# Fourier sums folded four ways, with the folds in the projection, and one block for the sample's and the prompt's Fourier part and the output projection

## The reference

```
h    = layer_norm(x) * (1 + sc1) + sh1
q, k, v, u = split(h @ w_in)                     # 512 columns each
o    = diff_attention(rope(q), rope(k), v)       # 4 heads of 128, then rms norm * gain
f    = fft2(u in 4 groups of 128, ortho).real    # over positions and group channels
f    = f @ w_fourier[group]
mix  = concat(o, f) @ w_out
x    = layer_norm(ALPHA * x + (1 + g1) * mix) * ln1_g + ln1_b
h    = layer_norm(x) * (1 + sc2) + sh2
x    = layer_norm(ALPHA * x + (1 + g2) * ((silu(h @ w_gate) * (h @ w_up)) @ w_down)) * ln2_g + ln2_b
```

## Time and profile before

| what | value |
|---|---|
| median of three runs | 3462.7 us (3454.75 to 3465.51) |
| profiled execution, its own time | 3461.79 us |
| its span | 3460.0 us |
| PE busy | 3147.7 us, 91% of the span |
| DVE busy | 1497.7 us, 43% |
| ACT busy | 1039.3 us, 30% |
| POOL busy | 1041.9 us, 30% |
| DMA | 309.29 MB, mean 89 GB/s |

### The profile page before, as it was taken

The page is one execution under the profiler, slowest core; times in us unless marked ns, Lnnn a source line. Parts: engine busy times, 40 slices in busy tenths (PEclk is TensorE's granted clock), DMA queues, the critical chain, the costliest instruction groups (busy, mean ns, idle before and its releaser), DMA issues.

```text
span 3460.0 us, 39737 instructions
## 1 busy us (share of the span) xinstructions
PE 3147.7 (91%) x15230; PEld 2628.0 (76%) x15230; DVE 1497.7 (43%) x2226; ACT 1039.3 (30%) x1592; POOL 1041.9 (30%) x589
## 2 busy tenths in 40 slices
PE   8799996999999967598599999979999998999995
PEld 1588884666666646477499999969999987999994
DVE  2343333888888734477521222171221245221225
ACT  1111112777777723223321211121121122111211
POOL 0122220011111110266443333373333345333333
PEclk9899998999999989799799999989999998999997
DMA  9222226121211032444431111232111213121111
GB/s 354 85 92 94 94 89 140 31 60 48 69 50 47 22 111 101 156 146 161 158 106 61 61 61 66 92 116 74 66 61 61 100 59 122 62 70 62 61 61 49
DMA packets 165031, 309.29 MB, mean 89 GB/s; under 512 B 12725, under 2 KB 100662, under 8 KB 162870
## 3 DMA queue, kind: packets, MB, share of 16 engines
q1 hardware_dynamic: 164922, 307.85, 27.0%
HBM read 241.69 MB, written 66.11 MB: 89 GB/s over the span
## 4 chain that ended last, share of the span: by engine, by line
PE 44%; POOL 3%; issue 2%; DVE 1%; POOLq 1%; ACT 0%; DMA 0%; DVEq 0%; SPq 0%; ACTq 0%
PE ffn_gu L1737 10%; PE ffn_gu L1738 10%; PE ffn_gu L1739 10%; PE ffn_dn L1753 5%; PE ffn_dn L1754 5%; PE ffn_dn L1755 5%; POOL ffn_out L1670 1%; POOL ffn_h_lo L1710 1%; POOL ffn_w_lo L1659 1%; POOLq L1665 1%; DVE ffn_out L1780 0%; DMA ffn_h_in<-scr_h_d 0%; POOL ffn_a_lo L1688 0%; DVE ffn_h_lo L1784 0%; ACT ffn_w_hi L1607 0%
## 5 line engine op out<-in xcount | busy, mean ns | idle before, releaser
L1737 PE MATMUL ffn_gu<-ffn_h_hi,ffn_w_hi 128*128 128x384 f32 x2112 | 707.3, 335 | 28.6 <-DVE ffn_h_lo L1784 25.5
L1739 PE MATMUL ffn_gu<-ffn_h_hi,ffn_w_lo 128*128 128x384 f32 x2112 | 706.9, 335 | 0.0
L1738 PE MATMUL ffn_gu<-ffn_h_lo,ffn_w_hi 128*128 128x384 f32 x2112 | 706.8, 335 | 0.0
L1659 POOL TENSOR_TENSOR ffn_w_lo<-ffn_w_raw,ffn_w_hi 128x2048 fp32r<-128x2048 f32 x99 | 461.0, 4657 | 405.7 <-ACT ffn_w_hi L1607 403.9
L1799 DVE TENSOR_TENSOR ffn_a_raw<-ffn_sil,ffn_gu 128x384 f32<-128x384 f32 x132 | 73.1, 554 | 949.2 <-PE ffn_gu L1739 949.2
L1737 PEld LDWEIGHTS ffn_gu<-ffn_h_hi,ffn_w_hi 128*128 128x128 f32 x2112 | 397.3, 188 | 30.8 <-issue 25.8
L1738 PEld LDWEIGHTS ffn_gu<-ffn_h_lo,ffn_w_hi 128*128 128x128 f32 x2112 | 397.3, 188 | 1.2
L1739 PEld LDWEIGHTS ffn_gu<-ffn_h_hi,ffn_w_lo 128*128 128x128 f32 x2112 | 397.3, 188 | 0.0
L1753 PE MATMUL ffn_dn<-ffn_w_hi,ffn_a_hi 128*128 128x512 f32 x792 | 315.4, 398 | 47.3 <-DVE ffn_total L1811 16.5
L1811 DVE TENSOR_TENSOR ffn_total<-ffn_total,ffn_dn 128x512 f32<-128x512 f32 x360 | 246.0, 687 | 229.8 <-PE ffn_dn L1755 229.8
L867 DVE TENSOR_REDUCE att_peak<-att_sc 128x1 f32<-128x1024 f32 x256 | 312.5, 1221 | 71.8 <-PE att_sc L693 65.9
(11 more groups left out here) (216 smaller groups left out, 4578.7 us busy)
## 6 DMA issues: line engine op xcount, KB each, us to landing
ffn_w_raw<-in_w_gu SPq DMA_DIRECT2D x132, 512.0 KB, 4.5
ffn_w_raw<-in_w_dn SPq DMA_DIRECT2D x66, 512.0 KB, 4.5
mod_wa<-in_w_ada SPq DMA_DIRECT2D x32, 768.0 KB, 7.0
att_q_t<-scr_qs_d SPq DMA_DIRECT2D x128, 128.0 KB, 2.9
proj_x_in<-in_x SPq DMA_DIRECT2D x18, 512.0 KB, 3.8
mix_x_in<-in_x SPq DMA_DIRECT2D x18, 512.0 KB, 4.0
scr_x_d<-mix_x SPq DMA_DIRECT2D x18, 512.0 KB, 4.7
scr_h_d<-mix_h SPq DMA_DIRECT2D x18, 512.0 KB, 5.5
```

The costliest lines, as they stand in the source:

```text
L1659: nc.gpsimd.tensor_tensor(w_lo[:, i, :], w_raw[:, i, :], w_hi[:, i, :].bitcast(F32), ALU.subtract).then_inc(wlo_done[i], 1)
L1737: nc.tensor.matmul(dst, w_hi[:, i, cols], h_hi[:, k, tokens], start=(k == 0), stop=False)
L1738: nc.tensor.matmul(dst, w_hi[:, i, cols], h_lo[:, k, tokens], start=False, stop=False)
L1739: m = nc.tensor.matmul(dst, w_lo[:, i, cols], h_hi[:, k, tokens], start=False, stop=(k == KD - 1))
```

## The change

The sample's rows are put in another order on the host (`sample_rows`; the rotary table and the output follow). Four consecutive tiles k of the sample then hold rows n, n + 1024, 1024 - n and 2048 - n (n below 512; for n = 0 the last two are rows 512 and 1536). `project` keeps u of four tiles, and DVE (`fold_even`) and POOL (`fold_odd`) add and subtract them into four operands, which go to `fold_d`; row 512 and a running sum for output position 1024 are kept apart (`b0_d`, `mid_d`). The Fourier sums of the sample are then 4 parts (even cosine, even sine, odd cosine, odd sine) of 4 chunks of 128 rows with tables of 512 columns, in place of 32 steps. Two chunks of the prompt come before them in the same list (`CHUNKS` = 18).

`attention` copies each finished quad twice out of `ring`, exact and rounded, and POOL subtracts; the hi and the lo part are stored. So the attention half of the mixed operand is loaded already split.

`fourier_sample`, `fourier_prompt` and `mix_out` become one block, `fourier_and_mix`. Its result of the Fourier part stays in SBUF. The load and split of `w_out` lie between the chunks. For the output projection the sample's tiles come first and the prompt's last. The attention half of a tile's product (`products(t, 0)`) doesn't wait for a split; the Fourier half (`products(t, 1)`) does. `x_in` and `x1_n` have one buffer in place of two, and the loops are written out. The tables' low parts are made by POOL in place of DVE.

The core of the diff:

```diff
...
+            def store_fold(k):
+                sp.wait_ge(odd_done, k + 1)
+                sp.wait_ge(mid_done, k + 1)
+                for part in range(4):
+                    whole = part == 1 or k
+                    sp.dma_start(fold_d[part, k, 0 if whole else 1:P, :], u[0 if whole else 1:P, part, :]).then_inc(fold_stored, 16)
+                if k == 0:
+                    for part, row in ((0, 0), (2, 1), (3, 3)):
+                        sp.dma_start(fold_d[part, 0, 0:1, :], pair[0:1, row, :]).then_inc(fold_stored, 16)
+                    sp.dma_start(b0_d, pair[0:1, 2, :]).then_inc(fold_stored, 16)
...
+                if t > PT and (t - PT) % 4 == 0:
+                    store_fold((t - PT) // 4 - 1)
...
+                if t > PT and (t - PT) % 4 == 0:
+                    act.wait_ge(fold_stored, 64 * ((t - PT) // 4 + 1))
+                nc.scalar.activation(u[:, t if t < PT else (t - PT) % 4, :], acc[:, 3, :], ACT.Copy).then_inc(u_done, 1)
...
+            def fold_odd(k):
+                pool.wait_ge(u_done, PT + 4 * (k + 1))
+                if k:
+                    pool.wait_ge(fold_stored, 64 * (k + 1))
+                nc.gpsimd.tensor_tensor(pair[:, 1::2, :], u[:, 0::2, :], u[:, 1::2, :], ALU.subtract).then_inc(minus_done, 1)
+                pool.wait_ge(minus_done, k + 1)
+                pool.wait_ge(plus_done, k + 1)
+                nc.gpsimd.tensor_tensor(u[:, 2, :], pair[:, 1, :], pair[:, 3, :], ALU.subtract)
+                nc.gpsimd.tensor_tensor(u[:, 3, :], pair[:, 1, :], pair[:, 3, :], ALU.add).then_inc(odd_done, 1)
+                pool.wait_ge(even_done, k + 1)
+                if k:
+                    pool.wait_ge(mid_done, k)
+                    nc.gpsimd.tensor_tensor(mid[:], mid[:], u[:, 0, :], ALU.add).then_inc(mid_done, 1)
+                else:
+                    nc.gpsimd.tensor_copy(mid[:], u[:, 0, :]).then_inc(mid_done, 1)
...
+            def fold_even(k):
+                dve.wait_ge(u_done, PT + 4 * (k + 1))
+                if k:
+                    dve.wait_ge(fold_stored, 64 * (k + 1))
+                nc.vector.tensor_tensor(pair[:, 0::2, :], u[:, 0::2, :], u[:, 1::2, :], ALU.add).then_inc(plus_done, 1)
+                dve.wait_ge(plus_done, k + 1)
+                dve.wait_ge(minus_done, k + 1)
+                nc.vector.tensor_tensor(u[:, 0, :], pair[:, 0, :], pair[:, 2, :], ALU.add)
+                nc.vector.tensor_tensor(u[:, 1, :], pair[:, 0, :], pair[:, 2, :], ALU.subtract).then_inc(even_done, 1)
...
+                    sp.wait_ge(flo_done, m + 1)
+                    for part, tile in ((0, f_hi), (1, f_lo)):
+                        src = tile[:, m % 2, :].bitcast(F32)
...
-                        nc.scalar.activation(f_out[:, m % 2, :], ring[:], ACT.Copy, scale=keep["subln_g"][:, 0:1]).then_inc(ring_read, 1)
+                            act.wait_ge(stored[m % 2], 32 * (m // 2))
+                        nc.scalar.activation(f_raw[:, m % 2, :], ring[:], ACT.Copy, scale=keep["subln_g"][:, 0:1])
+                        nc.scalar.activation(f_hi[:, m % 2, :], ring[:], ACT.Copy, scale=keep["subln_g"][:, 0:1]).then_inc(ring_read, 1)
...
+            def split_out(m):
+                pool.wait_ge(ring_read, place["z", m] + 1)
+                nc.gpsimd.tensor_tensor(f_lo[:, m % 2, :], f_raw[:, m % 2, :], f_hi[:, m % 2, :].bitcast(F32),
+                                        ALU.subtract).then_inc(flo_done, 1)
...
-def fourier_sample(nc, keep, u_d, w_f, chan, tab_s, four_d):
-def fourier_prompt(nc, keep, u_d, w_f, chan, tab_p, four_d):
-def mix_out(nc, keep, x, att_d, four_d, w_out, mod_rows, ln_g, ln_b, x1_d, h2_d):
...
+CHUNKS = PT + 4 * 4
...
+def fourier_and_mix(nc, keep, x, fold_d, b0_d, mid_d, up_d, w_f, chan, tab_p, tab_s, signs, att_d, w_out, mod_rows, ln_g, ln_b, x1_d, h2_d):
...
+        x_in = s.sb("x_in", [P, D])
+        x1_n = s.sb("x1_n", [P, D])
...
+        ORDER = list(range(PT, NT)) + list(range(PT))
...
+            def load_chunk(i):
+                part, k = chunk_place(i)
+                if i >= 3:
+                    sp.wait_ge(oplo_done, i - 2)
+                sp.dma_start(op_raw[:, i % 3, :], up_d[k] if part == PROMPT_SET else fold_d[part, k]).then_inc(op_landed[i % 3], 16)
+                if i >= 3:
+                    sp.wait_ge(tablo_done, i - 2)
+                sp.dma_start(tab_raw[:, i % 3, :], tab_p[k] if part == PROMPT_SET else tab_s[part, k]).then_inc(tab_landed[i % 3], 16)
...
+            def load_m(r):
+                if r >= 2:
+                    sp.wait_ge(acc_done, r - 1)
+                for part, tile in ((0, m_hi), (1, m_lo)):
+                    sp.dma_start(tile[:, r % 2, 0:HEADS, :].bitcast(F32),
+                                 att_d[part].rearrange("h c (t q) -> t c h q", q=P)[ORDER[r]]).then_inc(m_landed[r % 2], 16)
...
+            sp.dma_start(chan_in, chan.rearrange("t p c -> p t c")).then_inc(small_landed, 16)
+            sp.dma_start(wf_in.rearrange("p (g d) -> p g d", g=GROUPS), w_f.rearrange("g p d -> p g d")).then_inc(small_landed, 16)
+            load_chunk(0)
...
+            for i in range(1, CHUNKS):
+                load_chunk(i)
+                if i % 2 and i // 2 < KD:
+                    load_w(i // 2)
+                if i == 8:
+                    load_x(0)
+                    load_gate(1)
                     sp.dma_start(norm_b[:], ln_b.to_broadcast([P, D])).then_inc(row_landed, 16)
+                if i == 12:
+                    sp.wait_ge(chunk_used, PT + 1)
+                    load_m(0)
+                    load_m(1)
...
+            for r in range(NT + 2):
+                if r == ST:
+                    sp.wait_ge(gated, ST)
+                    load_gate(0)
+                if r + 1 < NT:
+                    load_x(r + 1)
+                if r + 2 < NT:
+                    load_m(r + 2)
...
+                for g in range(GROUPS):
+                    rows = slice(g * P, (g + 1) * P)
+                    dst = bank[:, base + g, :]
+                    stop = k == (PT - 1 if part == PROMPT_SET else 3)
+                    nc.tensor.matmul(dst, op_hi[:, i % 3, rows], tab_hi[:, i % 2, :], start=(k == 0), stop=False)
+                    nc.tensor.matmul(dst, op_hi[:, i % 3, rows], tab_lo[:, i % 2, :], start=False, stop=False)
+                    if part == 0 and k == 0:
...
+                        nc.tensor.matmul(dst, b0_hi[:, rows], across, start=False, stop=False)
+                        nc.tensor.matmul(dst, b0_lo[:, rows], across, start=False, stop=False)
+                    m = nc.tensor.matmul(dst, op_lo[:, i % 3, rows], tab_hi[:, i % 2, :], start=False, stop=stop)
+                m.then_inc(chunk_used, 1)
...
+            def products(t, half):
+                slot = t % 2
+                if half == 0:
+                    pe.wait_ge(m_landed[slot], 32 * (t // 2 + 1))
+                    if t < 2:
+                        pe.wait_ge(direct_done, 2 * GROUPS)
+                    else:
+                        pe.wait_ge(gated, t - 1)
+                else:
+                    pe.wait_ge(mlo_done, t + 1)
...
+            for i in range(CHUNKS):
+                sums(i)
+                if i == 0:
+                    mix_middle()
+                for part in (PROMPT_SET, 0, 1, 2):
+                    if i == last_chunk(part) + 2:
+                        mix_channels(part)
+            products(0, 0)
+            products(1, 0)
+            mix_channels(3)
+            products(0, 1)
+            products(1, 1)
+            for t in range(2, NT + 2):
+                if t < NT:
+                    products(t, 0)
+                    products(t, 1)
+                turn(t - 2)
...
+            def split_table(i):
+                pool.wait_ge(tabhi_done, i + 1)
+                nc.gpsimd.tensor_tensor(tab_lo[:, i % 2, :], tab_raw[:, i % 3, :], tab_hi[:, i % 2, :].bitcast(F32),
+                                        ALU.subtract).then_inc(tablo_done, 1)
...
+            def combine(par):
+                base = first_bank(2 * par + 1)
+                dve.wait_ge(direct_done, GROUPS * (par + 1))
+                for g in range(GROUPS):
+                    dve.wait_ge(mixed, GROUPS * (2 * par + 2) + g + 1)
+                    first = 1 - par
+                    near, far = slice(0, 256), slice(256 + first, 512)
+                    back = slice(511 - first, None if par else 0, -2)
+                    nc.vector.tensor_tensor(f_all[:, g, 0, par:512:2], direct[:, g, near], bank[:, base + g, near], ALU.subtract)
+                    nc.vector.tensor_tensor(f_all[:, g, 3, par + 2 * first:512:2], direct[:, g, first:256],
+                                            bank[:, base + g, first:256], ALU.add)
+                    nc.vector.tensor_tensor(f_all[:, g, 2, back], direct[:, g, far], bank[:, base + g, far], ALU.subtract)
```

(40 more changed lines are left out.)

773 lines of the change are left out of this document (328 added, 445 removed).

## The result

The changed kernel takes 3385.95 us (median, 3382.57 to 3388.22) against 3462.98 for the kernel before on the same chip: ratio 0.978, 95% interval 0.9763 to 0.9799. The profiled execution took 3382.57 us with a span of 3380.5. The forecast was 3367, range 3335 to 3415. The sum was not right term by term, though, and that is what follows.

The account below looks back on a forecast made before the run. PE was taken to bound projection and attention; 105 of 432 us in the merged blocks were waits and slow clock. -110.1 + 1 + 4.5 + 8.4 + 1.7 = -94.5 from 3461.8 gives 3367 us, range 3335 to 3415.

Parts of the forecast that it names:

- (e): Projection: folds cost 0 to 1.5 us at each of three tiles, 1 taken; last store lands 4.5 us later.
- (f): Attention: a second copy out of `ring` adds 14 x 0.6 = 8.4 us; at the end 1.7 us more.
- (a): Start of the new block: from its first issue through the middle row's sums, 10.1 us.
- (b): New block's chunks: 260 matmuls plus prompt channels, middle position and lower clock, 66.2 us.
- (c): Waits among the chunks for table splits, operand split, DMA and clock: 18 us, bounds 0 and 45.
- (d): End of the sums to first tile's products: attention halves, channels, wait for `combine(1)`, Fourier halves, 26.2 us.
- Tiles: Output projection: split of m goes off the path, 11.8 us a tile; 201.5 us in place of 228.9.
- rival 1: Output projection: tiles stay at 13.5 us; price 20 us, total 3387; chance 0.16.
- The rule weighed: Among the chunks: DVE instructions with two SBUF inputs and GpSimd's SBUF reads exclude each other; mostly hidden, at worst 6 us.
- 2 (feed-bound chunks): Fourier sums: chunks bound by loads and serial table instructions; price 27 us, total 3394; chance 0.14.
- 3 (serial stages): Output projection: single-buffered `x1_n` and `x_in` put stages in series, 22.4 us a tile, total 3547; chance 0.03.
- 4 (every attention step slower): Attention: second copy and POOL's split slow 64 steps by 0.5 us, 32 us, total 3391; chance 0.06.

Follow-up runs that it names:

- The experiment with two buffers: Operands and tables of the Fourier sums loaded into two buffers each in place of three, against the changed kernel with whole rows stored (3372.63 us): 3381.57 us.

## Why the prediction came out as it did

The forecast, 3367, was 19 us too low, and it came that near only because two errors of opposite sign offset each other, which is luck. Against its terms the losses came out 28.4 us larger (22.8 + 1.9 - 0.2 + 3.9) and the block's gain 14.3 larger. Of the rest, 0.8 us are the start and what lies behind the block, and 3.4 are the distance of the median from the profiled execution.

- **(e), the projection: the step that failed.** The text had "ACT's next copy of u waits for them, and PE wants that bank only 17 us on", and charged nothing for the stores; the 1 us of (e) was for the folds. That took a store of 127 rows to be as quick as one of 128. They had landed only 34.5 us after the first was issued (287.48 to ACT's copy at 321.98). This cost 16.8 us at that tile, and storing whole rows took 11.8 off the projection and 13.3 off the kernel. The second half, "that tile's rows are ready 0.5 us before PE wants them: 0 to 1.5 each", counted DVE's fold at its undisturbed length. In the trace two of its instructions took 1.81 and 1.77 us in place of 0.68, and it waited 3.61 us for POOL's first. So PE waited 2.0 us, and each of the three folds made its tile 2.2 us longer, at the full clock; in the kernels with whole rows the lower clock came on top behind one or two of them. The stall that the text named as a sign of error ("a stall of PE at each fold") did appear.
- **The end of the projection**, 4.5 forecast, 6.4 measured, within its bounds of 3 to 7.
- **(f), the second copy**: 14 x 0.6 = 8.4 forecast; 8.2 measured for the stretch, 8.1 by giving the ring back early. The mechanism and its size were right.
- **Attention's tail**: 1.7 forecast, 5.6 measured. The step that failed was "SP's two stores are in time": for the last quad they are not.
- **(a) the start** 10.1, measured 1296.79 - 1285.46 = 11.3. **(b) and (c)** 66.2 + 18, measured 68.0. The matmul count was right and the waits were mis-sized, 1.8 us (1.5 for the operand split, 0.3 for the table). The text took 237 GB/s as what the DMA can give; among the chunks single slices reach 387 and the mean is 217. The experiment with two buffers shows that the loads would have mattered without the third. The terms written for a late table (0.63 twice, 1.1, 2.37 and 1.1 to 1.2) also add up to 5.9 us, not 6.1. **(d) the end** 26.2, measured 1391.99 - 1364.76 = 27.2. Its wait for `combine(1)`, 5.6 against 5.52, is a hit by luck: the terms written, 5.6 less 3 plus 0.6 and 1.1, make 4.3. In the trace the combination began only 1.9 us before PE ran out of work.
- **Tiles**: 201.5 from the first tile's products to the last, measured 1592.7 - 1392.0 = 200.7. The late wait does what was said, if less evenly: with the early wait put back the kernel is 15.3 us slower, where rival 1 had 20, and about half of that is at tile 2. The text read the earlier trace rows as 0.5 us more for DVE's step when its sum of x is held up; the rows give 1.5 (the sum ends 4.4 us after the turn begins, not 2.9). That would have put the step at 12.1 us, above the 11.8 of a tile, yet PE never waited for it among the tiles. But two errors offset each other inside the 200.7. A tile is 12.1 us, not 11.8, because matmuls start (1592.72 - 1590.62) / 9 = 0.233 us apart and not 0.227, at the same granted clock of 2.4 GHz. In return 15 x 12.1 = 181.5 leaves 19.2 for the start, the end and late loads, where the text had 201.5 - 177 = 24.5. What slows the matmuls by 3% here was not tried.
- **The rule weighed** (SBUF — State Buffer, Who interferes with whom). Stretching was seen among the chunks (1502 ns for 683) and at the folds (1.81 us for 0.68), as that page of the Trainium skill says. Among the chunks it cost nothing, as the text had taken. The same stretching was overlooked in (e), where it stood right before PE.
- **Rivals.** 1 (tiles at 13.5) and 2 (feed-bound chunks) gave nearly the measured time, 3387 and 3394, for reasons that did not occur. 3 (serial stages) did not occur. 4 (every attention step slower) did not either: the 8 us went when the ring was freed earlier.

## What to carry to other kernels

Count the rows of every DMA, not only its bytes: leaving row 0 out turned a store of 128 rows into one of 127, which by its rate one DMA engine carries alone. Patch the odd row in SBUF and move whole tiles, or cut at a multiple of 16. Work added to an engine with much idle time is free only where that engine waits, so place it behind the instruction that the critical engine wants next; and when an accumulator has two readers, give it back after the first.

## What the runs showed of the hardware

- A store of 127 rows of 2 KB flows at 27 GB/s, one of 122 at 55, of 124 at some 105, of 125 at some 135; with the load behind it, all is moved 13.6 us after the issue for 127 rows and 4.1 for 128.
- The issuing engine stalls as well: SP took 9.85 us to issue a third store of 127 rows behind two others, and 11.04 for three one-row stores that took 0.86 elsewhere.
- A fold's instruction of 512 columns on DVE took 0.68 us alone and 1.8 beside POOL's.
- Behind a wait of 14.35 us PE started its matmuls 0.43 us apart, at 1.2 GHz. Behind waits of 2.0 to 2.6 us, with PE at work on either side, the granted clock stayed at 2.4 GHz in some cases and fell to 1.2 for 3.4 us in others, at the same place of the same projection code.
